# Gated delta stage: decay sums by split one-pass products in place of a native fp32 product

## The reference, cut to what matters

```python
dec = jnp.cumsum(g, axis=-1)                      # sums of log decays
gam = jnp.exp(jnp.where(incl, dec[..., :, None] - dec[..., None, :], -jnp.inf))
a_low = jnp.where(strict, jnp.einsum('bhnid,bhnjd->bhnij', kb, k) * gam, 0.0)
t_inv = triangular_solve(a_low + eye, eye)
u = t_inv @ vb
w = t_inv @ (kb * jnp.exp(dec)[..., None])
qk = jnp.einsum('bhnid,bhnjd->bhnij', q, k) * gam
```

## Time and profile before

| what | value |
|---|---|
| median of 3 runs | 2252.84 us (2252.02 to 2256.53) |
| the profiled execution's own time | 2254.09 us |
| its span, first to last instruction | 2252.3 us |
| PE busy | 2196.4 us, 98% of the span |
| DVE, ACT, POOL busy | 1500.4, 902.4, 1100.7 us |
| mean granted TensorE clock | 0.993 of full |
| gated delta stage | about 370 to 622 us, a trip is 61 us |

### The profile page before, as it was taken

One profiled execution on the slowest core, in us unless ns is written; L12 is line 12 of the kernel. 1 busy time (PEld: TensorE's weight loads), 2 busy tenths in 40 slices (PEclk: granted clock), 3 DMA queues, 4 the chain that ended last, 5 costly groups with the idle time before them and its releaser, 6 DMA issues.

```text
span 2252.3 us, 29708 instructions
## 1 busy us (share of the span) xinstructions
PE 2196.4 (98%) x10576; PEld 1838.2 (82%) x10576; DVE 1500.4 (67%) x3551; ACT 902.4 (40%) x1436; POOL 1100.7 (49%) x885
## 2 busy tenths in 40 slices
PE   8999988999999999999999999999999999999998
PEld 6888777988878888888888888888888888888885
DVE  4655697667645342197888888882349878788883
ACT  6555464444444333343333333332333333333343
POOL 3433244554423453246666666665337765555500
PEclk9999999999999999999999999999999999999999
DMA  4222242455252322234444444456479999999940
GB/s 174 78 92 77 73 145 87 140 181 167 70 191 94 128 97 96 83 117 150 140 146 148 141 146 149 140 169 227 140 271 374 392 370 344 364 347 355 363 158 38
DMA packets 168832, 403.35 MB, mean 179 GB/s; under 512 B 27648, under 2 KB 101632, under 8 KB 158368
## 3 DMA queue, kind: packets, MB, share of 16 engines
q1 hardware_dynamic: 133920, 334.77, 42.8%
q0 software_dynamic: 34816, 67.41, 8.1%
HBM read 336.84 MB, written 65.28 MB: 179 GB/s over the span
## 4 chain that ended last, share of the span: by engine, by line
PE 71%; DVE 1%; ACT 1%; issue 0%; DVEq 0%
PE ps L1476 13%; PE ps L174 11%; PE ps L176 11%; PE ps L175 11%; PE ps L2538 8%; PE ps L2536 8%; PE ps L2537 8%; PE ps L1809 1%; PE ps L2588 1%; PE ps L1559 0%; PE ps L2566 0%; ACT ffn_norm_scaled_sb L1700 0%; DVE h_sb L1519 0%; PE ps L1742 0%; ACT merge_high_sb L1434 0%
## 5 line engine op out<-in xcount | busy, mean ns | idle before, releaser
L2057 POOL DMA_INDIRECT g_dense<-up_gates_summed_sb,up_gate_at_sb x384 | 415.6, 1082 | 258.7 <-issue 214.7
L174 PE MATMUL ps<-n_high_sb,up_u_high_sb 128*128 128x512 f32 x1024 | 398.4, 389 | 0.0
L176 PE MATMUL ps<-n_high_sb,up_u_low_sb 128*128 128x512 f32 x1024 | 398.4, 389 | 0.0
L175 PE MATMUL ps<-n_low_sb,up_u_high_sb 128*128 128x512 f32 x1024 | 398.3, 389 | 0.0
L2536 PE MATMUL ps<-down_v_high_sb,down_w_high_sb 128*128 128x512 f32 x768 | 298.8, 389 | 0.0
L2538 PE MATMUL ps<-down_v_high_sb,down_w_low_sb 128*128 128x512 f32 x768 | 298.8, 389 | 0.0
L2537 PE MATMUL ps<-down_v_low_sb,down_w_high_sb 128*128 128x512 f32 x768 | 298.8, 389 | 0.0
L2456 ACT ACTIVATE down_v_high_sb<-down_v_sb 128x1024 fp32r<-128x1024 f32 x120 | 125.8, 1048 | 312.0 <-PE ps L2538 293.3
L1900 DVE TENSOR_TENSOR up_u_low_sb<-up_u_sb,up_u_high_sb 128x1024 fp32r<-128x1024 f32 x128 | 156.4, 1223 | 139.7 <-ACT up_u_high_sb L2076 132.3
L2278 POOL DMA_INDIRECT expert_rows_sb<-expert_v,chosen_expert_sb x128 | 156.7, 1224 | 165.3 <-DVE h_sb L2328 68.8
L2088 ACT ACTIVATE up_gelu_sb<-ps 128x512 f32<-128x512 f32 x128 | 76.5, 598 | 395.1 <-PE ps L176 268.7
(11 more groups left out here) (380 smaller groups left out, 4525.3 us busy)
## 6 DMA issues: line engine op xcount, KB each, us to landing
up_u_sb<-expert_u SPq DMA_DIRECT2D x128, 512.0 KB
down_v_sb<-expert_v SPq DMA_DIRECT2D x32, 2048.0 KB
a_dense<-up_gelu_sb SPq DMA_DIRECT2D x128, 256.0 KB
g_dense<-nought_sb SPq DMA_DIRECT2D x8, 3072.0 KB, 11.5
down_gelu_sb<-a_dense SPq DMA_DIRECT2D x32, 768.0 KB
down_gates_sb<-g_dense SPq DMA_DIRECT2D x32, 768.0 KB
w_slots_sb<-w_conv SPq DMA_DIRECT2D x19, 1024.0 KB, 4.8
decay_rows_sb<-decay_sum_rows SPq DMA_DIRECT2D x16, 512.0 KB, 4.4
```

Of the source, the lines that this page charges most:

```text
L174: pe.matmul(out, ah, bh, start=k == 0, stop=False)
L175: pe.matmul(out, ah, bl, start=False, stop=False)
L176: last = pe.matmul(out, al, bh, start=False, stop=k == n - 1)
L2057: pool.indirect_dma_start(cells, at, summed[:, tt, k:k + 1], None).then_inc(stored[tt], 16)
```

## The change

The log decays `g` are split once, by POOL at the stage's start, into a high part of type F32R (`g_high`) and a low part, the difference (`g_low`). The steps are made twice, from the high part (`steps`) and the low part (`steps_low`). The triangles of ones are copied once into F32R by DVE (`masks`). PE makes each sum with two one-pass products that add up in PSUM.

In trip 0 POOL makes a lane's high steps and then its low steps. In the later trips it makes all four lanes' high steps as before, and then the low steps, lane by lane, each waiting for `ks_done` of its lane: the low steps lie in the memory of `a_t` (`over=True`), whose last reader in the trip before is the product L1381. PE waits for `low_stepped` besides `stepped`, and once for the masks.

```diff
-    steps, e, at, qk = (per(x, [P, 4, P]) for x in ("steps", "decay", "a_t", "qk"))
+    steps, e = per("steps_high", [P, 4, P], F32R), per("decay", [P, 4, P])
+    steps_low = per("steps_low", [P, 4, P], F32R, over=True)
+    at, qk = (per(x, [P, 4, P]) for x in ("a_t", "qk"))
...
+    masks = beside_gates.take("gdn_step_masks", [P, 2, P], F32R)
+    g_high, g_low = (beside_gates.take(f"gdn_decay_{x}", [P, TT, 2 * GDN_H], F32R) for x in ("high", "low"))
...
         @block.gpsimd
         def _(pool):
+            g = m.decay[:, :, 32:32 + 2 * GDN_H]
+            pool.tensor_copy(g_high[:, :, :], g).then_inc(split, 1)
+            pool.wait_ge(split, 1)
+            pool.tensor_tensor(g_low[:, :, :], g, bits32(g_high[:, :, :]), ALU.subtract).then_inc(split, 1)
+            pool.wait_ge(split, 2)
+
+            def step(i, u, out, part, done):
+                hh, s = lanes[u]
+                for d in range(2):
+                    g = bits32(part[:, TS * s:TS * s + TS, block_of(i * HEADS + (hh + d * GDN_H), 1)]).broadcast_to([P, TS, P])
+                    last = pool.tensor_tensor(out[u][:, 2 * d:2 * d + 2, :], g, pair(sq(m, "ge" if d else "le")), ALU.mult)
+                last.then_inc(done[u], 1)
+
             for i in range(TRIPS):
                 for u in U:
-                    hh, s = lanes[u]
                     pool.wait_ge(summed[u], i + 1)
-                    for d in range(2):
-                        g = m.decay[:, TS * s:TS * s + TS, block_of(i * HEADS + (32 + hh + d * GDN_H), 1)].broadcast_to([P, TS, P])
-                        last = pool.tensor_tensor(steps[u][:, 2 * d:2 * d + 2, :], g, pair(sq(m, "ge" if d else "le")), ALU.mult)
-                    last.then_inc(stepped[u], 1)
+                    step(i, u, steps, g_high, stepped)
+                    if i == 0:
+                        step(i, u, steps_low, g_low, low_stepped)
+                for u in U if i else ():
+                    pool.wait_ge(ks_done[u], i + 1)
+                    step(i, u, steps_low, g_low, low_stepped)
...
         def _(dve):
...
+            for d, mask in enumerate(("gt", "lt")):
+                last = dve.tensor_copy(masks[:, d, :], sq(m, mask))
+            last.then_inc(masks_made, 1)
             dve.memset(nought[:, :], 0.0).then_inc(nought_made, 1)
...
         def _(pe):
...
+            pe.wait_ge(masks_made, 1)
             for i in range(TRIPS):
                 for u in U:
                     pe.wait_ge(out_done[u], i + 1)
                     pe.wait_ge(stepped[u], i + 1)
+                    pe.wait_ge(low_stepped[u], i + 1)
                     for d in range(2):
-                        last = pe.matmul(whole(u)[:, d * L:(d + 1) * L], sq(m, "lt" if d else "gt"),
-                                         steps[u][:, 2 * d:2 * d + 2, :].rearrange("p c n -> p (c n)"), start=True, stop=True)
+                        for n, part in enumerate((steps, steps_low)):
+                            last = pe.matmul(whole(u)[:, d * L:(d + 1) * L], masks[:, d, :],
+                                             part[u][:, 2 * d:2 * d + 2, :].rearrange("p c n -> p (c n)"), start=n == 0, stop=n == 1)
                     last.then_inc(summed[u], 1)
```

More of the change, by code:

```diff
@@ L1091, in gdn_stage, with per @@
     work = m.region(AT_WORK, AT_END - 4.25)
-    def per(name, shape):
+    def per(name, shape, dt=F32, over=False):
         size = 4 * int(np.prod(shape[1:]))
-        return [(spare if spare.at + size <= spare.end else work).take(f"gdn_{name}{u}", shape) for u in U]
+        rs = [Region(nc, r.at, r.end) for r in (spare, work)] if over else (spare, work)
+        return [rs[0 if rs[0].at + size <= rs[0].end else 1].take(f"gdn_{name}{u}", shape, dt) for u in U]
     halves = work.take("gdn_halves", [P, NL, P])
@@ L1126, in gdn_stage @@
     side = SideGates(m, "gdn", KT)
+    beside_gates = m.h_region()
+    beside_gates.at += 14 * KB
+    masks = beside_gates.take("gdn_step_masks", [P, 2, P], F32R)
+    g_high, g_low = (beside_gates.take(f"gdn_decay_{x}", [P, TT, 2 * GDN_H], F32R) for x in ("high", "low"))
+    split, masks_made, low_stepped = m.sem("gdn_decay_split"), m.sem("gdn_step_masks_made"), [m.sem(f"gdn_low_steps_made{u}") for u in U]
     AHEAD = 21
```

## The result

| | median | runs |
|---|---|---|
| before | 2256.02 us | 10, 2252.02 to 2257.51 |
| changed | 2260.03 us | 10, 2255.61 to 2262.52 |

The ratio is 1.0019, with a 95% interval of 1.0010 to 1.0027: some 4.3 us slower, while I had forecast +2.3 us and called it no change. The time lies 1 us above my range. The three runs of before shown ahead of the prediction had a median of 2252.84 us, all ten have 2256.02, so 3.2 of the 4.9 us between 2255.1 and 2260.03 are the reference's own level, and the rest, 1.7 us (2.0 by the ratio), is the change's.

The account below looks back on a forecast made before the run. PE looked like the stage's bound, but DVE's chain, waiting on POOL's masks, ended each trip's head. Trip 0 +2.9 us and heads -0.6 gave +2.3 on a median of 2252.84: 2255.1 us, range 2250.5 to 2259.0.

Parts of the forecast that it names:

- The sums: PE's sums at each trip's head: sixteen one-pass products at 0.120 us take 1.92 instead of 3.45 us, saving 1.53 a trip.
- The tail: Trips 1 to 3: POOL's low steps end near 434.9, 3.7 us before the sums, leave DVE undisturbed and cost nothing.
- The head: Head of trips 1 to 3: DVE still waits out POOL's masks, so 0.2 us gained a trip, 0.6 in all.
- the boundary: Third mask's start, 2.95 us after the first's; lane 0's L1265, at 2.89, catches or misses it; a miss was forecast.
- The rival of the catch: L1265 catches the boundary in trips 1 to 3, gaining the whole 1.53 us each: -1.7 us, 2251.1 us, chance 0.30.
- Trip 0: No tail hides POOL's added steps: masks 3.3 us late, longer half clock, 4.6 us late less 1.7 given back, +2.9 us.
- the fall of the clock in the kernel before: Trip 0: half clock from 390.0 to 393.5 after 1.83 us idle, costing 1.7 us; the change was expected to remove it.
- a rival that needs two falls or three: Trips 1 to 3: PE's 2.0 us idle brings clock falls, up to 1.7 us each; three give +7.4, 2260.2 us; chance 0.12.

Follow-up runs that it names:

- e7: Changed kernel with trip 0 as in the kernel before and DVE making all four lanes' masked products before the two-operand instructions; 2252.53 us, ratio 0.9982.
- e6: Kernel before with DVE making all four lanes' masked products before the two-operand instructions; 2255.82 us, ratio 1.0000.
- e8: As e7, with ACT rounding the gate weights before the key and query copies in trips 1 to 3; 2250.00 us, ratio 0.9976.
- e10: Kernel before with the DVE and ACT reorderings of e8, native products throughout; 2255.60 us, ratio 1.0002.
- e2: Changed kernel with trip 0 as in the kernel before: plain steps, native products, split and mask copies moved later; 2256.08 us, ratio 1.0004.
- e3: Changed kernel with trip 0 as in the kernel before and the first gate product repeated seven times in trips 1 to 3; 2252.77 us, ratio 0.9993.
- e9: Changed kernel with extra unused PE products before the sums in trip 0, seven for the first lane, four for each other; 2256.61 us, ratio 1.0010.
- e1: Changed kernel with the first gate product repeated seven times in trips 1 to 3, filling PE's idle; 2257.70 us, ratio 1.0010.
- e4: Kernel before with eight more POOL steps in trip 0, results unused but waited for by the sums, products native; 2257.25 us, ratio 1.0009.
- e5: Changed kernel with DVE making all four lanes' masked products before the two-operand instructions; 2258.15 us, ratio 1.0009.

## Why the prediction was wrong, step by step

*The sums.* Right: 16 x 0.12, 1.99 us with the first product's longer start, from 3.45.

*The tail.* Right: low steps made from 433.00 on in 4.63 us and over at 437.63, 3.9 us ahead of the sums at 441.48, as the timeline of POOL shows:

```profile
433.00 4.63 POOL L1237 TENSOR_TENSOR gdn_steps_low_sb<-gdn_decay_low_sb,squares_sb 128x256 fp32r<-128x256 f32 x8 [0.18 <-PE ps L1409]
```

The DVE instructions beside them were not disturbed: L1325 (once L1300) took 340 to 343 ns in all trips, and L1322 (once L1297) 340 to 351, as its line shows (min/median/max ns, first and last start):

```profile
L1322 DVE SCALAR_TENSOR_TENSOR gdn_first_part_sb<-ps,gdn_neg_decay_sb,channels_sb x32: 340/343/351, 433.1 to 621.7; 128x128 f32<-128x128 f32 x32
```

*The head.* Right: L1265 missed the boundary and the gain was 0.16 us in the head, 0.24 in the whole trip, where I had 0.2. One detail differed: the first masked product waited for the first mask (ended at 445.02), not for ACT's copy. The rival of the catch did not happen. What stood between PE's 1.5 us and the trip is shown in two steps: with L1265 and L1267 out of the masks' way 1.1 us arrive (e7 against e6), and with L825 ahead of the first mask as well all 1.5 (e8 against e10).

*Trip 0.* The mechanism was right and its times were right to 0.5 us, counted from the stage's start, and the +2.9 us came out as +2.3 between the two profiled executions. What I treated as fixed was the fall of the clock in the kernel before, whose 1.7 us I credited to the change. e2 and e3 (66.5 and 66.8 us) have trips 0 of the old kind without that fall. Where it does not come, trip 0 costs 4.3 us. That the kernel before had it in the one execution that both sides of this difference lean on is luck; over the timed executions e2 puts trip 0 at 3.4 us.

*The step that failed* is the sum's last one, how the clock in trips 1 to 3 entered. I wrote that PE's 1.5 us becomes idle and that "just such an idle share" stood before the fall at 390.0, and then set it beside the sum as a rival that needs two falls or three, chance 0.12, with a single one left to the range, instead of putting it in the sum with a share of trips. It is the term that was mis-sized: I took 0 falls, and in the three executions profiled with this idle unfilled (changed, e2, e9) 5 of 9 later trips had one, each 1.5 to 1.7 us (62.42 - 60.77, 66.53 - 65.00). That is 5/9 x 3 x 1.6 = 2.7 us an execution. With it my sum is 2.3 + 2.7 = 5.0 us; with trip 0 and the trips' gain as profiled it is 2.3 - 3 x 0.24 + 2.7 = 4.3, which is what the ratio shows, though with so few trips behind the 5/9 this closeness is luck in part. The timed experiments split the 4.3 us another way: 3.4 for trip 0 (changed less e2, forecast 2.9), 2.0 for the falls (changed less e1, forecast 0) and -1.6 for the rest (e3, forecast -0.6), each good to 2 or 3 us. In both ways, by the middle values, the term that was put at nothing is the largest miss. No fall stands in the 27 later trips of the other profiled kernels, whose idle before the turns was 0.4 to 0.9 us: twelve with native sums (before, e4, e6, e10), six with the idle filled (e1, e3), nine with DVE's new order (e5, e7, e8).

*The level.* My range was set on a median of three runs; ten gave 3.2 us more. On the level of ten the same range would have ended at 2262.2 us, above the measured time; so the level put the time outside, and the clock term made the change 4.3 us instead of 2.3.

What stays open: why the same idle is followed by half clock in one trip and not in the next. The executions show both cases with PE's idle time alike to 0.1 us; no run here tells more.

## What to carry to other kernels

When an engine's work is shortened and another chain sets the end, the saving turns into idle of that engine, and on TensorE this idle is itself a cost where the granted clock has been seen to fall after such a stretch: put it in the sum, with the share of repeats in which it may come. Before shortening TensorE, look for two-operand DVE instructions that start beside GpSimd work; here two reorderings that were worth nothing alone made the change worth 1.5 us a trip. The first trip of a loop has no tail before it, so work that hides in the tail needs a first trip of its own.

## What the runs showed of the hardware

Adding TensorE work made kernels faster: 21 products of 512 columns took the median from 2256.08 to 2252.77 us (e3 against e2), 19 took 1.5 us off trip 0 (e9), in both cases with the granted clock at its 2.4 GHz level where it had been at 1.2 GHz. DVE instructions with two SBUF operands grew from 0.43 to 1.56 us beside GpSimd's masks, while the 32 with one SBUF tensor and PSUM that now have GpSimd's steps beside them stayed between 340 and 351 ns. The Trainium skill, SBUF — State Buffer, at the single rule on the shared port pair, says that a DVE instruction with two SBUF inputs contends with a GpSimd instruction that reads SBUF, and that one with at most one SBUF input does not, outside the two-port modes. The runs agree in the main. One detail stays open: in trip 0 L1290 took 0.46 us, although by the records the last mask ended 0.18 us after its start.
